# Inverse roots and gates from one ScalarE table in a two-network kernel

## The reference

```python
def rms_norm(x, g, eps=NORM_EPS):
    y = xf * lax.rsqrt(jnp.mean(xf * xf, axis=-1, keepdims=True) + eps)
...
# dsa_mixer: q = rope(rms_norm(q, q_gain), pos), the same for k
# rwkv7_mixer
    w = -jax.nn.softplus(-(w0 + jnp.tanh(d_w) @ w_decay_up)) - 0.5
    decay = jnp.exp(-jnp.exp(w.astype(f32)))
    a = jax.nn.sigmoid((a0 + d_a @ w_aicl_up).astype(f32))
    kk = kk / jnp.maximum(jnp.sqrt(jnp.sum(kk * kk, axis=-1, keepdims=True)), 1e-12)
...
    y = ((y - mu) * lax.rsqrt(var + GN_EPS)).reshape(B, S, RWKV_WIDTH)
...
# hybrid_layer
    q_a = l2norm(q) * (DN_DK ** -0.5)          # x * rsqrt(sum(x * x) + EPS), the same for k_a
    o_a = o_a * lax.rsqrt(jnp.mean(o_a * o_a, axis=-1, keepdims=True) + EPS) * dn_norm_w
    y_b = o_b * jax.nn.silu(bz)
```

## Time and profile before

| | |
|---|---|
| median of the runs | 3554.79 us (3554.66 to 3555.49) |
| profiled execution | 3555.32 us, span 3553.6 us |
| mean granted clock of TensorE | 0.957 of full |
| PE, DVE, ACT busy | 3234.6, 2117.6, 1614.1 us |
| table loads on ACT | 132, 1.28 us each |
| reciprocals of 512 columns on DVE | 16, 3.35 us each |
| weight stream | 538 MB, a mean of 153 GB/s for all traffic |

### The profile page before, as it was taken

One profiled execution on the slowest core, in us unless ns is written; L12 is line 12 of the kernel. 1 busy time (PEld: TensorE's weight loads), 2 busy tenths in 40 slices (PEclk: granted clock), 3 DMA queues, 4 the chain that ended last, 5 costly groups with the idle time before them and its releaser, 6 DMA issues.

```text
span 3553.6 us, 61781 instructions
## 1 busy us (share of the span) xinstructions
PE 3234.6 (91%) x23552; PEld 3024.8 (85%) x23552; DVE 2117.6 (60%) x2839; ACT 1614.1 (45%) x2118; POOL 225.7 (6%) x202
## 2 busy tenths in 40 slices
PE   6988888879899999999798899889988899999998
PEld 6888787868799987777688888888878899999998
DVE  5756665554545588888565655565554555555554
ACT  4444444433333467777444434444433444444443
POOL 0011111110000000000011001110110100000001
PEclk9999999989999999999899999999998999999999
DMA  5422222213446689999333333333323455555553
GB/s 183 142 74 79 79 73 73 73 44 125 120 146 183 198 300 353 327 327 361 127 110 96 125 102 107 102 125 102 101 95 127 163 170 180 178 182 181 180 182 136
DMA packets 231209, 544.69 MB, mean 153 GB/s; under 512 B 16768, under 2 KB 98944, under 8 KB 231040
## 3 DMA queue, kind: packets, MB, share of 16 engines
q1 hardware_dynamic: 229664, 537.99, 45.4%
q0 software_dynamic: 656, 2.49, 0.2%
q10 hardware_dynamic: 720, 1.74, 0.1%
HBM read 540.05 MB, written 2.10 MB: 153 GB/s over the span
## 4 chain that ended last, share of the span: by engine, by line
PE 55%; issue 28%; DVE 11%; ACT 5%; POOL 0%; DVEq 0%; ACTq 0%; POOLq 0%
PE gp L441 14%; PE gp L442 14%; PE gp L443 14%; PE pm L492 4%; ACT w_hi L1063 3%; DVE w_lo L1506 2%; PE pm L501 2%; PE pm L505 1%; DVE arena L1673 1%; PE pm L480 1%; DVE arena L1528 1%; PE pm L983 0%; DVE h_both L1518 0%; DVE arena L1715 0%; DVE arena L1763 0%
## 5 line engine op out<-in xcount | busy, mean ns | idle before, releaser
L1506 DVE TENSOR_TENSOR w_lo<-stage,w_hi 128x1024 fp32r<-128x1024 f32 x1018 | 1251.0, 1236 | 949.3 <-ACT w_hi L1063 934.8
L1063 ACT ACTIVATE w_hi<-stage 128x1024 fp32r<-128x1024 f32 x1018 | 1071.0, 1056 | 884.8 <-PE gp L443 671.8
L441 PE MATMUL gp<-h_both,w_hi 128*128 128x256 f32 x4432 | 1305.7, 295 | 78.7 <-DVE w_lo L1506 32.5
L442 PE MATMUL gp<-h_both,w_hi 128*128 128x256 f32 x4432 | 1274.6, 288 | 0.0
L443 PE MATMUL gp<-h_both,w_lo 128*128 128x256 f32 x4432 | 1273.6, 287 | 0.0
L441 PEld LDWEIGHTS gp<-h_both,w_hi 128*128 128x128 f32 x4432 | 871.5, 197 | 102.9 <-issue 49.4
L442 PEld LDWEIGHTS gp<-h_both,w_hi 128*128 128x128 f32 x4432 | 872.0, 197 | 2.4 <-issue 1.7
L443 PEld LDWEIGHTS gp<-h_both,w_lo 128*128 128x128 f32 x4432 | 871.0, 197 | 0.0
L441 PE MATMUL gp<-y_both,w_hi 128*128 128x256 f32 x1024 | 292.5, 286 | 0.6 <-DVE y_both L1518 0.6
L442 PE MATMUL gp<-y_both,w_hi 128*128 128x256 f32 x1024 | 291.7, 285 | 0.0
L443 PE MATMUL gp<-y_both,w_lo 128*128 128x256 f32 x1024 | 291.5, 285 | 0.0
(11 more groups left out here) (481 smaller groups left out, 4077.7 us busy)
## 6 DMA issues: line engine op xcount, KB each, us to landing
stage<-in_stream SPq DMA_DIRECT2D x1018, 512.0 KB, 4.1
x<-in_x SPq DMA_DIRECT2D x4, 512.0 KB, 8.7
out<-arena SPq DMA_DIRECT2D x4, 512.0 KB, 2.6
arena<-in_lora POOLq DMA_DIRECT2D x8, 192.0 KB, 2.7
c<-in_c POOLq DMA_DIRECT2D x1, 896.0 KB, 5.4
c<-in_c ACTq DMA_DIRECT2D x1, 704.0 KB, 10.3
c<-in_c ACTq DMA_DIRECT2D x1, 640.0 KB, 7.8
vecs<-in_vecs ACTq DMA_DIRECT2D x1, 184.0 KB, 5.4
```

Source lines behind the costliest of these rows:

```text
L441: T.matmul(o, w_hi[:, slot, w], hi[:, k, :], start=first[t], stop=False)
L442: T.matmul(o, w_hi[:, slot, w], lo[:, k, :], start=False, stop=False)
L1063: A.activation(w_hi[:, slot, :], stage[:, k, :], ACT.Copy).then_inc(s_hi, 1)
L1506: V.tensor_tensor(w_lo[:, slot, :], stage[:, sub % SLOTS, :], w_hi[:, slot, :].bitcast(F32), ALU.subtract).then_inc(s_lo, 1)
```

## The change

- Every inverse root is now Ln and then Exp with a scale of -0.5 on ACT, with the scale of the mean and the epsilon inside the Ln, which reads PE's sum in PSUM. DVE's scaling and reciprocal are gone. This holds for the five norms, the query and key norms of both networks, the two head norms. The key norm of the recurrent mixer keeps its lower bound: DVE writes the maximum with 1e-24 first.
- The sigmoid gates of the recurrent mixer are Exp(-x), Ln(1 + .), Exp(-.) on ACT, both gates in one 512-column operation; `w0` is negated once in place. `r_a` moves to lie beside `r_lw`.
- The Silu of the sliding-window gate becomes a Copy at the eviction, three ACT operations between feeds 18 and 19, and one product on DVE.
- The table set that holds both Ln and Exp is named and loaded by hand ahead of the first norm, the loops, once in each delta turn (behind its Silu), and ahead of later norms.
- Where an Ln now stands on ACT, it waits for PE's sum at that place of ACT's program: in the recurrent mixer that of `d_rs` ahead of feed 3, in the delta part that of `n_rn` behind feed 4.

```diff
@@ -21,6 +21,7 @@
...
 TOPK = 64
+LN_EXP = "natural_log_exp_and_others"
@@ -1083,9 +1086,14 @@
...
+            def inverse_root(n):
+                act.wait_ge(sem("s_nsum"), n + 1)
+                A.activation(n_rs, pm[:, 4, 0:S], ACT.Ln, scale=1.0 / D, bias=eps[:, 0:1]).then_inc(sem("s_nrv"), 1)
+                act.wait_ge(sem("s_nrv"), n + 1)
+                A.activation(n_rs, n_rs, ACT.Exp, scale=-0.5).then_inc(sem("s_nrs"), 1)
+
             def norm(n, last=False):
-                act.wait_ge(sem("s_nrv"), n + 1)
-                A.activation(n_rs, n_rs, ACT.Sqrt).then_inc(sem("s_nrs"), 1)
+                inverse_root(n)
@@ -1093,6 +1101,8 @@
...
+            A.preload_act_table_set(LN_EXP)
+            act.wait_ge(sem("s_eps"), 1)
@@ -1186,17 +1196,23 @@
...
                 act.wait_ge(sem("s_lora_in"), 5 + p)
-                A.activation(r_lw, pm[:, 0, 0:S], ACT.Sigmoid, bias=vec("w0", p))
-                A.activation(r_a, pm[:, 1, 0:S], ACT.Sigmoid, bias=vec("a0", p)).then_inc(sem("s_rw_sig"), 1)
+                A.activation(r_lw, pm[:, 0, 0:S], ACT.Exp, scale=-1.0, bias=vec("w0", p))
+                chain.link(A.activation(r_a, pm[:, 1, 0:S], ACT.Exp, scale=-1.0, bias=vec("a0", p)))
+                chain.link(A.activation(r_gates, r_gates, ACT.Ln, bias=1.0))
+                A.activation(r_gates, r_gates, ACT.Exp, scale=-1.0).then_inc(sem("s_rw_sig"), 1)
                 A.activation(r_g, pm[:, 2, 0:S], ACT.Copy).then_inc(sem("s_rw_g"), 1)
-                act.wait_ge(sem("s_rw_kkn"), p + 1)
-                A.activation(r_tmp, pm[:, 3, 0:S], ACT.Sqrt).then_inc(sem("s_rw_nrm"), 1)
+                act.wait_ge(sem("s_rw_kkm"), p + 1)
+                A.activation(r_tmp, r_tmp, ACT.Ln).then_inc(sem("s_rw_nrm"), 1)
+                act.wait_ge(sem("s_rw_nrm"), 2 * p + 1)
+                A.activation(r_tmp, r_tmp, ACT.Exp, scale=-0.5).then_inc(sem("s_rw_nrm"), 1)
...
                 A.activation(r_lw, r_lw, ACT.Exp).then_inc(sem("s_rw_exp"), 1)
+                act.wait_ge(sem("s_qk_ss"), p + 1)
+                A.activation(d_rs, pm[:, 4, :], ACT.Ln, scale=1.0 / P, bias=eps[:, 0:1]).then_inc(sem("s_qk_rv"), 1)
@@ -1206,7 +1222,7 @@
...
                 act.wait_ge(sem("s_qk_rv"), p + 1)
-                A.activation(d_rs, d_rs, ACT.Sqrt).then_inc(sem("s_qk_rs"), 1)
+                A.activation(d_rs, d_rs, ACT.Exp, scale=-0.5).then_inc(sem("s_qk_rs"), 1)
@@ -1223,16 +1239,20 @@
...
                 A.activation(r_Y[:, 2:4, :], r_Y[:, 0:2, :], ACT.Square).then_inc(sem("s_rw_yc2"), 1)
+                act.wait_ge(sem("s_rw_var"), p + 1)
+                A.activation(r_tmp, pm[:, 4, 0:S], ACT.Ln, scale=1.0 / 64, bias=eps[:, 1:2]).then_inc(sem("s_ho_rv"), 1)
                 act.wait_ge(sem("s_ho_rv"), p + 1)
-                A.activation(r_tmp, r_tmp, ACT.Sqrt).then_inc(sem("s_ho_rs"), 1)
+                A.activation(r_tmp, r_tmp, ACT.Exp, scale=-0.5).then_inc(sem("s_ho_rs"), 1)
...
             act.wait_ge(s_zero, 6)
-            loop(act, RWKV_P - 1, rwkv)
-            rwkv(RWKV_P - 1, True)
+            act.wait_ge(sem("s_eps"), 2)
+            A.preload_act_table_set(LN_EXP)
+            chain.loop(RWKV_P - 1, 2, rwkv)
+            chain.turn(2, lambda i: rwkv(i, True), RWKV_P - 1)
@@ -1246,8 +1266,7 @@
...
             square(15)
-            act.wait_ge(sem("s_nrv"), 2)
-            A.activation(n_rs, n_rs, ACT.Sqrt).then_inc(sem("s_nrs"), 1)
+            inverse_root(1)
@@ -1373,7 +1393,7 @@
...
                     o = n_raw[:, j - 6, 3:S + 3] if j < 10 else n_z[:, j - 10, :]
-                A.activation(o, gp[:, j % 3, 0:S], ACT.Silu if j == 5 else ACT.Copy).then_inc(s_evac[j % 3], 1)
+                A.activation(o, gp[:, j % 3, 0:S], ACT.Copy).then_inc(s_evac[j % 3], 1)
@@ -1390,9 +1410,12 @@
...
                 A.activation(n_z, n_z, ACT.Silu).then_inc(sem("s_dn_z"), 1)
+                A.preload_act_table_set(LN_EXP)
...
                 feed2(4, i, last)
+                act.wait_ge(sem("s_qk_ss"), DSA_H + i + 1)
+                A.activation(n_rn, pm[:, 0, :], ACT.Ln, bias=eps[:, 0:1]).then_inc(sem("s_qk_rv"), 1)
@@ -1400,7 +1423,7 @@
...
                 act.wait_ge(sem("s_qk_rv"), DSA_H + i + 1)
-                A.activation(n_rn, n_rn, ACT.Sqrt).then_inc(sem("s_qk_rs"), 1)
+                A.activation(n_rn, n_rn, ACT.Exp, scale=-0.5).then_inc(sem("s_qk_rs"), 1)
@@ -1421,9 +1444,11 @@
...
                 ins.then_inc(sem("s_dn_os"), 1)
+                act.wait_ge(sem("s_dn_os"), i + 1)
+                A.activation(n_or, n_ss, ACT.Ln, scale=1.0 / P, bias=eps[:, 0:1]).then_inc(sem("s_ho_rv"), 1)
+                act.wait_ge(sem("s_ho_rv"), RWKV_P + i + 1)
                 feed2(16, i, last)
-                act.wait_ge(sem("s_ho_rv"), RWKV_P + i + 1)
-                A.activation(n_or, n_or, ACT.Sqrt).then_inc(sem("s_ho_rs"), 1)
+                A.activation(n_or, n_or, ACT.Exp, scale=-0.5).then_inc(sem("s_ho_rs"), 1)
@@ -1431,6 +1456,10 @@
...
                 feed2(18, i, last)
+                act.wait_ge(s_evac[2], EV_T2[2] + 4 * i + 2)
+                chain.link(A.activation(w_sg, w_z, ACT.Exp, scale=-1.0))
+                chain.link(A.activation(w_sg, w_sg, ACT.Ln, bias=1.0))
+                A.activation(w_sg, w_sg, ACT.Exp, scale=-1.0)
@@ -1451,8 +1480,8 @@
...
             act.wait_ge(s_zero, 8)
-            chain.loop(DN_H - 1, 1, turn2)
-            chain.turn(1, lambda i: turn2(i, True), DN_H - 1)
+            chain.loop(DN_H - 1, 3, turn2)
+            chain.turn(3, lambda i: turn2(i, True), DN_H - 1)
@@ -1518,9 +1548,6 @@
...
             def norm(n, gain, last=False):
-                dve.wait_ge(sem("s_nsum"), n + 1)
-                link(V.tensor_scalar(n_rs, pm[:, 4, 0:S], 1.0 / D, EPS, ALU.mult, ALU.add))
-                V.reciprocal(n_rs, n_rs).then_inc(sem("s_nrv"), 1)
@@ -1550,9 +1577,13 @@
...
+            V.memset(eps[:, 0:1], EPS)
+            V.memset(eps[:, 1:2], GN_EPS).then_inc(sem("s_eps"), 1)
...
             dve.wait_ge(sem("s_vecs"), 16)
+            V.tensor_scalar(vecs[:, VEC["w0"]:VEC["w0"] + 16], vecs[:, VEC["w0"]:VEC["w0"] + 16], -1.0, None,
+                            ALU.mult).then_inc(sem("s_eps"), 1)
@@ -1692,6 +1723,8 @@
...
+                dve.wait_ge(sem("s_rw_kkn"), p + 1)
+                V.tensor_scalar(r_tmp, pm[:, 3, 0:S], 1e-24, None, ALU.max).then_inc(sem("s_rw_kkm"), 1)
@@ -1710,9 +1743,7 @@
...
                 V.scalar_tensor_tensor(rk, r_mix[:, 0, :], vec("r_k", p), kp, ALU.mult, ALU.mult)
-                dve.wait_ge(sem("s_rw_nrm"), p + 1)
-                link(V.tensor_scalar(r_tmp, r_tmp, 1e-12, None, ALU.max))
-                link(V.reciprocal(r_tmp, r_tmp))
+                dve.wait_ge(sem("s_rw_nrm"), 2 * p + 2)
@@ -1723,10 +1754,6 @@
...
                 feed1(4, p, last)
-
-                dve.wait_ge(sem("s_qk_ss"), p + 1)
-                link(V.tensor_scalar(d_rs, pm[:, 4, :], 1.0 / P, EPS, ALU.mult, ALU.add))
-                V.reciprocal(d_rs, d_rs).then_inc(sem("s_qk_rv"), 1)
@@ -1758,9 +1785,6 @@
...
                 V.tensor_tensor(rk, pm[:, 3, S:2 * S], r_mix[:, 2, :], ALU.mult)
-                dve.wait_ge(sem("s_rw_var"), p + 1)
-                link(V.tensor_scalar(r_tmp, pm[:, 4, 0:S], 1.0 / 64, GN_EPS, ALU.mult, ALU.add))
-                V.reciprocal(r_tmp, r_tmp).then_inc(sem("s_ho_rv"), 1)
@@ -1769,8 +1793,8 @@
...
             dve.wait_ge(s_zero, 6)
-            chain.loop(RWKV_P - 1, 20, rwkv)
-            chain.turn(20, lambda i: rwkv(i, True), RWKV_P - 1)
+            chain.loop(RWKV_P - 1, 16, rwkv)
+            chain.turn(16, lambda i: rwkv(i, True), RWKV_P - 1)
@@ -1792,9 +1816,6 @@
...
             V.memset(m8be, -MARK)
-            dve.wait_ge(sem("s_nsum"), 2)
-            link(V.tensor_scalar(n_rs, pm[:, 4, 0:S], 1.0 / D, EPS, ALU.mult, ALU.add))
-            V.reciprocal(n_rs, n_rs).then_inc(sem("s_nrv"), 1)
@@ -2023,9 +2044,6 @@
...
-                dve.wait_ge(sem("s_qk_ss"), DSA_H + i + 1)
-                link(V.tensor_scalar(n_rn, pm[:, 0, :], EPS, None, ALU.add))
-                V.reciprocal(n_rn, n_rn).then_inc(sem("s_qk_rv"), 1)
@@ -2071,9 +2089,6 @@
...
                 feed2(15, i, last)
-                dve.wait_ge(sem("s_dn_os"), i + 1)
-                link(V.tensor_scalar(n_or, n_ss, 1.0 / P, EPS, ALU.mult, ALU.add))
-                V.reciprocal(n_or, n_or).then_inc(sem("s_ho_rv"), 1)
@@ -2112,6 +2127,7 @@
...
                 V.tensor_tensor(w_p1, w_l1[:, 0:S], w_l1[:, S:2 * S], ALU.add)
+                V.tensor_tensor(w_z, w_z, w_sg, ALU.mult)
@@ -2129,8 +2145,8 @@
...
             dve.wait_ge(s_zero, 8)
-            chain.loop(DN_H - 1, 10, turn2)
-            chain.turn(10, lambda i: turn2(i, True), DN_H - 1)
+            chain.loop(DN_H - 1, 8, turn2)
+            chain.turn(8, lambda i: turn2(i, True), DN_H - 1)
...
             def project(u0):
```

(10 more changed lines are left out.)

## The result

The changed kernel takes 3461.86 us, median of four runs (3459.1 to 3462.39), against 3554.72 before: a ratio of 0.9738 (95% interval 0.9721 to 0.9755), 92.9 us faster. The forecast was 78.4. The profiled execution took 3462.39 us with a span of 3460.4, and the mean granted clock is 0.970 in place of 0.957. There are 50 table loads in place of 132.

What follows compares the result with a forecast made beforehand. PE, busy 91%, was taken as the bound, losing time to waits for DVE chains and a lower clock. Mixer -47.6, norms -8.0, delta -24.6, window +3.2, last turn -1.4 sum to -78.4: 3476 us, own range 3465 to 3488, wide 3459 to 3507.

Steps and rivals of the forecast that it cites:

- A: End of a mixer turn: root 1.6 us sooner, PE's wait before L601 vanishes, -1.6 us six times.
- B: Mixer up to the transposes: DVE's chain shorter, -1.85 us in turns 1 to 6, -0.3 in turn 0, -1.4 last.
- C: Mixer, L480 to L501: a clock that holds gives -4.85 us a turn; three quarters taken, -25 in seven turns.
- D: The five norms: root takes 1.1 us where it took 2.70, -1.6 us each, -8.0 in all.
- E: Second network's delta part, L924 to L932: PE runs through in 7.4 us without DVE's reciprocal, -24.6 us.
- F: Sliding window part: the gate's product on DVE lengthens PE's longest wait, +0.4 us in eight turns, +3.2.
- G: Last turn of the second network: a Silu load goes and DVE is earlier before L480, -1.4 us.
- 1: Rival: the clock does not come back between L480 and L501; 3501 us, chance 0.17.
- Rival 4: The named table is not kept and each Ln and Exp brings a load again; 3564 us, chance 0.06.
- Rival 2: The clock holds throughout, in the last turns too; 3465 us, chance 0.11.
- Rival 3: ScalarE's longer chains delay w_hi and put back half of the 78 us; 3515 us, chance 0.08.

Runs made afterwards that it cites:

- Experiment 6: Changed kernel with the recurrent mixer's gates by Sigmoid again and the named table loaded again behind them: 3462.49 us.
- experiment 3: Changed kernel with DVE's scaling and reciprocal back for the recurrent mixer's query and key norm alone: 3488.78 us.
- experiment 5: Kernel before the change with only the recurrent mixer's query and key root by Ln and Exp from the named table: 3547.47 us.
- Experiment 4: Changed kernel with DVE's reciprocal back for the recurrent mixer's key norm alone: 3476.97 us.
- Experiment 9: Changed kernel with query/key scaling behind the solver's first additions, the window gate's product ahead of the softmax wait, the third norm's load behind its squares: 3453.90 us.
- experiment 2: Changed kernel with one more table load at nine places, 72 loads more (122 in all), reciprocals still gone: 3501.91 us.
- Experiment 1: Changed kernel with all wide reciprocals back on DVE, Ln and Exp kept on ACT, no table loads added: 3559.13 us.
- 8: Changed kernel with DVE's scaling of queries and keys moved behind the solver's first two additions: 3454.12 us.
- 10: Kernel of Experiment 9 with the window part's softmax sums, reciprocal and scaling ahead of the w_lo of feeds 20 and 21: 3423.65 us.
- experiment 7: Changed kernel with DVE's key-norm reciprocal back and two more small DVE steps in the same chain: 3488.90 us.

## Why the prediction was right, step by step

The mechanism was right: waits of PE for DVE's chains, and the clock behind them. The sum was 14.5 us short, 11.3 of them in the mixer. The 3461.9 us lie outside the forecast's own range (3465 to 3488), and inside the wide one (3459 to 3507) by 3 us.

- **A, -9.6 forecast, -13.0 measured** for L501 to the next L601 in seven turns. The wait of 1.6 vanished as said, but the boundary to the last turn shrinks as well (7.09 to 5.22), the stretch from turn 0 into turn 1 gave 2.5, and the others 0.13 more each. The end of the last turn gave 1.4, where I had 0.2.
- **B, -11.4 forecast, -17.4 measured** for L601 to L480 in turns 0 to 6. This is the most mis-sized term, and in it the chain's part: 2.5 us shorter and not 1.85, because DVE's 0.6 wait for w_hi went as well, so that nothing was left before L480 where I kept 0.6. In turn 0 the clock had fallen for 3.4 us before (169.0 to 172.4) and did not after, 1.5 us that I had not seen. The last turn gave 0.3 and not 1.4. My slack of 0.2 us at the gates was too small. They start 1.6 us before L604 (L601), where their load started with it and they themselves 1.2 behind it. Two loads left ACT's row ahead of them, at L1184 and L1189, and I had taken off only the second. Experiment 6 uses up 1.4 of the 1.65 us and costs nothing.
- **C, -25 forecast, -27.4 measured** in turns 0 to 6. The size is right, in part by luck. I had weighed a clock that holds against one that stays low as before, at three quarters. In fact the long fall was gone from all seven turns. Three held the clock (9.1, as worked out), and four had a short fall inside the solver and took 10.5 to 10.7. The waits there were misread too: before there was one of 0.88 for L1667 in each of turns 0 to 6 and not two of 0.9, and after there is one of 0.72 for POOL and one of 1.44 for L1698, behind which the four falls come. Of the cause I wrote only half. Experiments 3 and 5 show that the clock falls behind either of the two waits of 2.3 to 2.4 us, so that both had to go: one alone was worth 7.5 us, as the last of the two 27 (25.9 of them from 480 to 501 in the trace of experiment 3). Experiment 4 has a wait of 1.7 in all seven turns, and one fall behind it. The last turn lost 0.5, which I had at nothing.
- **D, -8.0 forecast, -7.5 measured.** It is 1.74 us a norm, for the terms 2.70 and 0.95 that are in the rows. But the load ahead of the third norm stands before its squares, with nothing to cover it, and cost 1.16 of that again. I had put it under idle time without looking at this norm. Experiment 9 takes it back.
- **E, -24.6 forecast, -24.8 measured** (84.1 to 59.3; 7.4 in each turn, as forecast). The load behind Silu (1833.01) costs nothing on PE's path, as said.
- **F, +3.2 forecast, +2.6 measured** (0.33 a turn). By the trace of experiment 9 it was avoidable: with the product in an idle stretch of DVE the wait is back at 3.7.
- **G, -1.4 forecast**, -2.0 measured from L501 to L983 in the last turn.
- **Not in the sum:** L932 to L983 in the other seven turns of the second network gave 2.5. Before, the clock fell inside the solver in three of them (62.0 us), and after in one; a turn in which it holds takes 61.1.

Of the rivals, 1 (no clock back) and 4 (the table not kept; 50 loads say otherwise) fell. (Rival 4 also has the loads of a mixer turn before as four; there were seven, L1165 and L1184 to L1227.) Rival 2 gave 3465 and is nearest in time, for another reason: the clock did not hold throughout. Rival 3 did not occur in the change, but experiment 2 is its mechanism: when ACT gets 1.28 us more at these places, w_hi comes late and it costs 40 us. For most of the removed loads I had put nothing into the sum. Experiment 1 bears that out while the reciprocals stand beside them, but these left too.

Open: what exactly makes the clock fall inside the solver in some turns and not in others that have the same waits. The number of such turns differs between traces with the same waits there (four in the changed kernel, three in experiment 6), and executions of one kernel differ by 3 to 15 us. That the falls make this difference is likely, and not shown.

## What to carry to other kernels

Price an edit against the kernel in which its neighbours are already gone: when two engines take turns in a chain, what one hides of the other comes out once it leaves, and two savings that are worth 0 and 53 us alone are worth 93 together. After each gain read again which wait ends last: the two moves that paid here (8 and 10) cost nothing but a place further down or up in DVE's program. And move what an engine does for later feeds behind what another engine waits for now.

## What was not expected of the hardware

- The same wait does not always have the same effect on the clock. Right behind PE's wait before the transposes it fell in one turn of seven at 1.7 us (experiment 4), in four of six at 1.8 (experiment 7), in six of six at 2.05 (experiment 2), and at 2.4 in four of six before and in five of five in experiment 5. In turn 2 of the kernel before it stayed at 0.50 from 353.4 to 367.1, though PE was busy for 12.7 of these 13.7 us.
- A load of the same table set that is already there is made all the same, at 1.28 us each (experiment 2, 72 of them).
